# A hybrid GLA, differential-attention and PEER trunk: scores by map, value projection beside the key drain, GLA sums first and roots in pairs

## The chip, the cores and the metric

The kernel runs on one core of one Trainium2 chip. The metric is the time of one execution in device microseconds; the median of three runs is given. One execution was also taken with the profiler.

## What is computed

One layer of a streaming encoder, float32, width 1024, for 1024 prompt tokens and 32 decode tokens (with 512 cached keys). Shared weights, two streams of conditioning.

```
h = rmsnorm(x) * gain * (1 + sc1) + sh1
gq, gk, gv, gr, glr, dq, dk, dv, gates = split(h @ w_in)
# mixer A: gated linear attention, 4 heads (dk 128, dv 256)
b = cumsum(log_sigmoid(glr @ w_alpha + b_alpha) / 16)
o_a = causal((q e^b)(k e^-b)^T) v + (q e^b) state;  state = e^b_last state + (k e^(b_last - b))^T v
y_a = (rmsnorm(o_a) * silu(gr)) @ w_gla_out
# mixer B: differential attention, 8 heads, two maps of 64 per head, values of 128
q, k = rope(rmsnorm(dq)), rope(rmsnorm(dk))       # k and dv are also outputs
p = softmax(q1 k1^T / 8, block-causal by 64) - lam * softmax(q2 k2^T / 8, same mask)
y_b = (rmsnorm(p v) * 0.8) @ w_diff_out
x = x + gt1 * ((sigmoid(g_a) y_a + sigmoid(g_b) y_b) @ w_out)
# PEER: per token 8 heads x top 16 of 128^2 experts by product keys
x = x + gt2 * sum_k softmax(score)_k gelu(h2 . u[idx_k]) v[idx_k]
```

## The kernel before, in words

The nine token tiles (eight of 128, one of 32) form five groups: tile 0, then tiles 1-2, 3-4, 5-6 and 7-8. For each group a *lane* of ticks runs all layers up to the product keys: norm, key projection and rotation ("dk"), value projection ("dv"), two passes of GLA with two heads each ("gq", "gk", "la", "gv", "gla", "gr"), query projection ("dq"), attention ("at"), merge, output projection, second norm and product keys. After that each token needs 128 expert rows. They come in 528 batches of two gathers, 1 MB each, into a ring of nine slots: `dots(b)` on DVE (L1657) multiplies the rows with the tokens, ACT applies gelu (L1212), `weigh(b)` makes a diagonal on DVE (L1668) and sums on PE (L886), which frees the two slots for POOL's next gathers (L1711).

`ticks(g)` lists the lane of a group with a cost for each tick. `sequence()` places them: the whole lane of group 0 and the first 14 ticks of group 1 (`EARLY`) stand ahead of the first gather, the latter beside the expert selection of tile 0; then come the two `unit` items (SP fetches a unit's tokens and indices) and the batches. The lane of group g+1 is spread over the batches in proportion to its costs: group 1 over batches 0 to 47, group 2 over 48 to 167, and so on; the last 120 or so batches have no lane beside them. `order(engine)` turns that into one program order for each engine, so every engine, SP's DMA queue too, takes the ticks in the same order and waits in place for its semaphores. PE has the lane's ticks and then `weigh(b-1)`; DVE `dots(b)`, `weigh(b-1)`, then the ticks; ACT half of the ticks, `dots(b)`, the rest.

The parts that the change touches:
- *Ticks* (L162 to 167). A dk tick i makes one projected tile on PE (`tokens`, L624) while i < 4 nt (nt tiles in the group); the square is on ACT a tick later (L986), the rotation's sums on DVE (L1339 to 1359), root and scaling (L1367) one and two later, PE's transposes (L660) one more, ACT's copies (L1006) and SP's stores (L1797 the rotated keys, L1808 their transpose) after that. So there are six ticks without a projection (the drain). A dv tick makes one tile on PE (L624), a copy on ACT (L1016), two stores. Weights lie in three slots of 1 MB; when the last tile of a unit is done, SP issues the load of three units later (L1737) and waits for PE first.
- *Banks.* PE takes PSUM banks 0 to 5 in turn (`take`, ALL). A GLA output goes to bank 2 or 5.
- *Scores* (`attend` on PE, L795). Map 0 reads partitions 0 to 63, map 1 partitions 64 to 127, each into its own two banks (`pair[m]`). Where a unit or the one before has more than 512 keys ("wide", every unit of groups 2 to 4), the scores wait for the exponentials of the unit just before; else for those of one earlier. Keys come in chunks of 512. DVE then sets a corner to a large negative number (L1503) and takes the maximum (L1504) of each map; ACT takes the exponentials (L1151).
- *GLA* on ACT: tick k copies the transposed key of unit k-2 (L1079), squares the output of unit k-3 (L1087), takes Ln and Exp of its mean (L1090, L1091: the root), then the decays of unit k (L1107 to L1112). On DVE: scaling of unit k-4's output by the root (L1405), which frees its bank, state update of k-3 (L1413), mask of k-2 (L1419), keyed products of k-1 (L1429 to 1434), and last the running sum of unit k (L1440, L1443). On PE: outputs and state product of k-2 (L715, L716, L721), the block products of k-1 (L729) and a transpose (L734). A stage has 2 nt units (in group 4: two units of tile 7, then two of tile 8) and four more ticks.

## Time and profile before

| | |
|---|---|
| median of 3 runs | 4257.27 us (4254.24 to 4258.38) |
| the profiled execution | 4264.31 us |
| its span, first to last instruction | 4262.5 us |
| mean granted TensorE clock | 0.802 of full |
| busy: PE, DVE, ACT, POOL | 3112.3, 2708.3, 1513.0, 1253.3 us |
| moved by DMA | 1499 MB, of which the gathers 1107 MB |
| mean DMA rate | 352 GB/s |

Busy times are averages over very different stages. Until 440 us nothing is gathered; then the lanes of groups 1 to 4 run beside the batches, at some 12 us per batch for group 1 and 7 us for the others; the last stretch has gathers alone, at some 5 us per batch. A releaser is what ended the idle time before an instruction.

### The profile page before, as it was taken

To read this page: it belongs to the slowest core of one execution; us is meant where nothing else is said; L and a number is where in the kernel's file an instruction comes from. 1 tells how busy PE (TensorE), PEld (TensorE's weight loads), DVE (VectorE), ACT (ScalarE), POOL (GpSimd) and SP (SyncE) were. 2 spreads that over 40 slices of the span, in tenths; PEclk is the share of its full clock that TensorE was granted. 3 is DMA by queue.
4 is the path that set the end of the run, shared out by engine and by line. 5 is a ranking of instruction groups with operands and counts; after the bars stand their busy time and mean duration, and the time that the engine had idled before them with its cause. 6 is when DMAs were issued, how large, how long until landed. Compare 5 with 4: busy or idle time off the path is not lost. (4 is left out here: it accounts for less than half of the span.)

```text
span 4262.5 us, 48896 instructions
## 1 busy us (share of the span) xinstructions
PE 3112.3 (73%) x15864; PEld 1989.7 (47%) x15864; DVE 2708.3 (64%) x7617; ACT 1513.0 (35%) x3085; POOL 1253.3 (29%) x1068
## 2 busy tenths in 40 slices
PE   6787688898788769788887679788776676633333
PEld 4676565676555327555554347454442364400000
DVE  1326357437667884578568874596678845776775
ACT  3533366312255651113555540133456611010010
POOL 0000112112233332333233332333333323354453
PEclk8798888899888779899878789888787788855555
DMA  7485767788989989999889899999999999999997
GB/s 263 142 323 188 285 237 260 270 312 336 361 342 373 359 313 398 394 417 404 352 353 361 335 368 385 414 399 400 382 387 383 373 414 413 396 415 415 414 404 329
DMA packets 269366, 1499.19 MB, mean 352 GB/s; under 512 B 44969, under 2 KB 81673, under 8 KB 97465
## 3 DMA queue, kind: packets, MB, share of 16 engines
q0 software_dynamic: 152064, 1107.36, 65.1%
q1 hardware_dynamic: 117048, 388.70, 24.2%
q8 instruction: 128, 2.10, 0.2%
q14 instruction: 126, 1.02, 0.1%
HBM read 1463.49 MB, written 31.36 MB: 351 GB/s over the span
## 5 line engine op out<-in xcount | busy, mean ns | idle before, releaser
L1711 POOL DMA_INDIRECT rt_ring<-in_peer_uv,rt_few_idx x1056 | 1250.0, 1184 | 2979.8 <-PE rt_acc L886 2344.6
L1657 DVE SCALAR_TENSOR_TENSOR rt_ring<-rt_ring,rt_h 128x1024 f32<-128x1024 f32 x1056 | 1267.6, 1220 | 541.2 <-DMA rt_ring<-in_peer_uv,rt_few_idx 536.6
L886 PE MATMUL rt_acc<-rt_ring,rt_diag 128*32 128x512 f32 x4224 | 762.4, 797 | 602.3 <-DVE rt_diag L1668 600.4
L635 PE MATMUL pair<-dense,w 128*128 128x256 f32 (+2 forms) x3056 | 599.4, 355 | 25.8 <-DMA w<-in_weights 24.2
L635 PEld LDWEIGHTS pair<-dense,w 128*128 128x128 f32 x3056 | 518.2, 198 | 140.7 <-issue 62.9
L624 PE MATMUL pair<-w,dense 128*128 128x256 f32 (+1 forms) x2352 | 557.8, 395 | 7.0 <-DVE dense L1313 2.8
L1212 ACT ACTIVATE rt_act_dot<-rt_dot 128x2 f32<-128x2 f32 x528 | 106.0, 202 | 1271.7 <-DVE rt_ring L1657 1262.5
L886 PEld LDWEIGHTS rt_acc<-rt_ring,rt_diag 128*32 128x32 f32 x4224 | 100.9, 122 | 930.1 <-DVE rt_diag L1668 789.3
L624 PEld LDWEIGHTS pair<-w,dense 128*128 128x128 f32 (+1 forms) x2352 | 437.5, 189 | 159.1 <-issue 73.7
L1668 DVE TENSOR_SCALAR rt_diag<-cst,rt_act_dot,rt_few_prob 128x32 f32<-128x32 f32 x1056 | 266.2, 297 | 82.6 <-ACT rt_act_dot L1212 64.1
L635 PE MATMUL bank<-dense,w 128*128 128x256 f32 (+2 forms) x1424 | 276.0, 350 | 1.4 <-DMA w<-in_weights 0.9
L635 PEld LDWEIGHTS bank<-dense,w 128*128 128x128 f32 x1424 | 236.1, 193 | 57.0 <-issue 31.5
L624 PE MATMUL bank<-w,dense 128*128 128x256 f32 (+1 forms) x1104 | 261.6, 394 | 0.2 <-DVE dense L1405 0.2
L624 PEld LDWEIGHTS bank<-w,dense 128*128 128x128 f32 (+1 forms) x1104 | 204.5, 188 | 67.9 <-issue 29.0
L1212 ACT ACT_TABLE_LOAD x171 | 219.4, 1283 | 3.0
L795 PE MATMUL pair<-w,dense 64*128 64x512 f32 (+5 forms) x416 | 124.8, 722 | 107.2 <-ACT dense L1151 99.7
L729 PE MATMUL pair<-dense 128*128 128x16 f32 (+1 forms) x528 | 98.8, 334 | 89.0 <-DVE dense L1434 89.0
L815 PE MATMUL bank<-w,dense 128*128 128x128 f32 (+2 forms) x640 | 130.6, 360 | 29.7 <-DVE dense L1472 28.3
L729 PEld LDWEIGHTS pair<-dense 128*128 128x128 f32 (+1 forms) x528 | 101.2, 289 | 105.3 <-issue 102.5
L815 PEld LDWEIGHTS bank<-w,dense 128*128 128x128 f32 (+2 forms) x640 | 107.8, 245 | 69.8 <-issue 67.4
L1151 ACT ACTIVATE dense<-pair,negmax 128x128 f32<-128x128 f32 (+8 forms) x144 | 104.8, 731 | 65.8 <-PE bank L770 47.4
L795 PEld LDWEIGHTS pair<-w,dense 64*128 64x128 f32 (+1 forms) x416 | 47.7, 235 | 158.8 <-issue 156.4
(241 smaller groups left out, 3314.5 us busy)
## 6 DMA issues: line engine op xcount, KB each, us to landing
w<-in_weights SPq DMA_DIRECT2D x284, 1024.0 KB
rt_ring<-in_peer_uv,rt_few_idx POOLq DMA_INDIRECT x1056
dense<-scratch_mod SPq DMA_DIRECT2D x18, 512.0 KB, 11.0
dense<-in_x_prompt SPq DMA_DIRECT2D x16, 512.0 KB, 10.3
rt_h<-scratch_h SPq DMA_DIRECT2D x33, 128.0 KB
rt_x<-scratch_x SPq DMA_DIRECT2D x132, 32.0 KB
out_k_prompt<-dense SPq DMA_DIRECT2D x32, 128.0 KB
out_v_prompt<-dense SPq DMA_DIRECT2D x32, 128.0 KB
```

The costliest lines, as they stand in the source:

```text
L624: mm = nc.tensor.matmul(bank[b][0:n, 0:CH], src[:, k, c0:c0 + n], wt[:, k * CH:(k + 1) * CH], start=(k == 0), stop=(k == KC - 1))
L635: mm = nc.tensor.matmul(bank[b][:, 0:n], wt[:, k * CH + j * P:k * CH + (j + 1) * P], src[:, k, 0:n], start=(k == 0), stop=(k == KC - 1))
L729: mm = nc.tensor.matmul(bank[b][0:n, i * GBLK:(i + 1) * GBLK], k_blk[:, i, 0:n], e_blk[:, x % 2, i * GBLK:(i + 1) * GBLK], start=True, sto ...
L795: mm = nc.tensor.matmul(pair[m][0:n, o + c:o + c + w], qd[rows, h, c0:c0 + n], keys_of[rows, c:c + w], start=True, stop=True)
L815: mm = nc.tensor.matmul(bank[5][0:n, 0:VD], mixT[0:w, G % 2, (kt - first) * P:(kt - first) * P + n], v[0:w, kt, :], start=(kt == 0), stop= ...
L886: mm = nc.tensor.matmul(acc[u % 2][a * T:(a + 1) * T, :], diag[b % 2][:, i, :], slot[:, D + c * BANK:D + (c + 1) * BANK], start=(q == 0), ...
L1151: nc.scalar.activation(prob[0:n, x % 2, m, 0:nk], pair[m][0:n, o:o + nk], ACT.Exp, bias=negmax[0:n, x % 2, m:m + 1], accum_out=total[0:n, ...
L1212: nc.scalar.activation(act_dot[:, b % 2, :], dot[:, b % 2, :], ACT.Gelu).then_inc(gelued, 1)
L1657: dt = nc.vector.scalar_tensor_tensor(up, up, 1.0, h2[u % 2][:], ALU.mult, ALU.mult, accum_out=dot[:, b % 2, i:i + 1])
L1668: dg = nc.vector.tensor_scalar(diag[b % 2][:, i, :], stack, act_dot[:, b % 2, i:i + 1], few_prob[u % 2][:, q * B + i:q * B + i + 1], ALU.m ...
L1711: nc.gpsimd.indirect_dma_start(ring[n % RING][:], None, d["peer_uv"], bass.IndirectOffsetOnAxis(ap=few_idx[u % 2][:, c:c + 1], axis=0)).th ...
```

## The change

In `ticks`, all dk projections come first, then dv ticks and the six draining dk ticks alternate. A GLA output's bank is one of 2, 5 and 4 in turn. Scores are made map by map, each map waiting for its own exponential. On ACT the square of unit k-3 goes behind the decays of unit k, and Ln and Exp are made for two units at once. On DVE the running sum is first in the tick, and two units' outputs are scaled in every odd tick. The same instructions remain, apart from half of the Ln and Exp operations and their table loads. (The words "early requests" in the change's name refer to nothing in the diff.)

```diff
@@ -159,12 +159,12 @@
         for kind in ("modrow", "modcol"):
             out.extend(((kind, part), 0.5) for part in range(2))
     add("norm", nt + 2, 4.5)
-    for kind in ("dk", "dv"):
-        lag = 6 if kind == "dk" else 2
-        for i in range(4):
-            for ti in range(nt):
-                out.append(((kind, g, i * nt + ti), 3.6 if kind == "dk" else 3.0))
-        out.extend(((kind, g, 4 * nt + i), 1.0) for i in range(lag))
+    out.extend((("dk", g, i), 3.6) for i in range(4 * nt))
+    for i in range(max(4 * nt + 2, 6)):
+        if i < 4 * nt + 2:
+            out.append((("dv", g, i), 3.0 if i < 4 * nt else 1.0))
+        if i < 6:
+            out.append((("dk", g, 4 * nt + i), 1.0))
     for p in range(2):
         for kind in ("gq", "gk"):
             out.extend(((kind, g, p, j), 3.0) for j in range(2))
@@ -710,7 +710,7 @@
                     if x < 2 and t == NT:
                         pe.wait_ge(st_in, 16 * (p + 1))
                     v = gv[0:n, ti, j * GDV:(j + 1) * GDV]
-                    bo, before = take(("go", g, p, t, j), [(2, 5)[(base + x) % 2]])
+                    bo, before = take(("go", g, p, t, j), [(2, 5, 4)[(base + x) % 3]])
                     pe.wait_ge(bank_free[bo], before)
                     nc.tensor.matmul(bank[bo][0:n, 0:GDV], attn[0:n, x % 2, 0:n], v, start=True, stop=False)
                     nc.tensor.matmul(bank[bo][0:n, 0:GDV], q_cum[:, x % 2, 0:n], s, start=False, stop=True).then_inc(bank_made[bo], 1)
@@ -782,16 +782,15 @@
                         slot = (g, "kv", kv_load_of(g, x))
                         keys_of = weights(slot)
                     wide = nk > BANK or (x > 0 and key_count(GROUPS[g][units[x - 1][1]]) > BANK)
-                    for m in range(2):
-                        pe.wait_ge(at_exped[m], base + max(0, x if wide else x - 1))
                     o = BANK * (x % 2) if nk <= BANK else 0
                     if x == 0:
                         b, before = sessions["dqT", g, 3, 1]
                         pe.wait_ge(bank_free[b], before + 1)
-                    for c in range(0, nk, BANK):
-                        w = min(BANK, nk - c)
-                        for m in range(2):
-                            rows = slice(m * HD, (m + 1) * HD)
+                    for m in range(2):
+                        rows = slice(m * HD, (m + 1) * HD)
+                        pe.wait_ge(at_exped[m], base + max(0, x if wide else x - 1))
+                        for c in range(0, nk, BANK):
+                            w = min(BANK, nk - c)
                             mm = nc.tensor.matmul(pair[m][0:n, o + c:o + c + w], qd[rows, h, c0:c0 + n], keys_of[rows, c:c + w],
                                                   start=True, stop=True)
                             if c + w == nk:
@@ -1077,18 +1076,6 @@
                     b, before = sessions["kt", g, p, t, j]
                     act.wait_ge(bank_made[b], before + 1)
                     nc.scalar.activation(k_tok[0:n, x % 2, :], bank[b][0:n, 0:P], ACT.Copy).then_inc(bank_free[b], 1)
-                if 0 <= k - 3 < len(units):
-                    x = k - 3
-                    ti, t, c0, n, j = units[x]
-                    c = x % 2
-                    b, before = sessions["go", g, p, t, j]
...
-                    act.wait_ge(gl_squared, base + x + 1)
-                    settle(nc.scalar.activation(gln[0:n, c:c + 1], gms[0:n, c:c + 1], ACT.Ln, bias=eps[0:n, :]))
-                    nc.scalar.activation(grstd[0:n, c:c + 1], gln[0:n, c:c + 1], ACT.Exp, scale=-0.5).then_inc(gl_rstd, 1)
                 if k < len(units):
                     ti, t, c0, n, j = units[k]
                     c = k % 2
@@ -1112,6 +1099,19 @@
                         ex = nc.scalar.activation(e_key[:, c, OFF[i]:OFF[i + 1]], cum[:, c, 1:GBLK * (i + 1) + 1], ACT.Exp,
                                                   scale=-1.0, bias=cum[:, c, GBLK * i:GBLK * i + 1])
                     ex.then_inc(gl_decays, 1)
+                if 0 <= k - 3 < len(units):
+                    x = k - 3
+                    ti, t, c0, n, j = units[x]
+                    c = x % 2
+                    b, before = sessions["go", g, p, t, j]
+                    act.wait_ge(bank_made[b], before + 1)
+                    act.wait_ge(gl_squared, base + x)
+                    nc.scalar.activation(gsq[0:n, :], bank[b][0:n, 0:GDV], ACT.Square, scale=GDV ** -0.5,
+                                         accum_out=gms[0:n, c:c + 1]).then_inc(gl_squared, 1)
+                    if c == 1:
+                        act.wait_ge(gl_squared, base + x + 1)
+                        settle(nc.scalar.activation(gln[0:n, :], gms[0:n, :], ACT.Ln, bias=eps[0:n, :]))
+                        nc.scalar.activation(grstd[0:n, :], gln[0:n, :], ACT.Exp, scale=-0.5).then_inc(gl_rstd, 2)
 
             def gla_gate(g, p, i):
                 nt, u = len(GROUPS[g]), i - 1
@@ -1397,8 +1397,18 @@
                             dve.wait_ge(kt_out[i], 16 * (g + 1))
                         settle(nc.vector.memset(k_blk, 0.0))
                         settle(nc.vector.memset(cum, 0.0))
-                if 0 <= k - 4 < len(units):
-                    x = k - 4
+                if k < len(units):
+                    ti, t, c0, n, j = units[k]
+                    c = k % 2
+                    if k >= 2:
+                        dve.wait_ge(gl_decays, base + k - 1)
+                    settle(nc.vector.tensor_tensor_scan(cum[:, c, 1:n + 1], one[:].to_broadcast([P, n]), glT[:, j, c0:c0 + n],
+                                                        0.0, ALU.mult, ALU.add))
+                    start = cum[:, c, 0:n].rearrange("p (b c) -> p b c", c=GBLK)[:, :, 0:1].to_broadcast([P, n // GBLK, GBLK])
+                    nc.vector.tensor_tensor(blk[:, c, 0:n].rearrange("p (b c) -> p b c", c=GBLK),
+                                            cum[:, c, 1:n + 1].rearrange("p (b c) -> p b c", c=GBLK), start,
+                                            ALU.subtract).then_inc(gl_blocked, 1)
+                for x in range(k - 5, k - 3) if k % 2 == 1 and 0 <= k - 5 < len(units) else ():
                     ti, t, c0, n, j = units[x]
                     b, before = sessions["go", g, p, t, j]
                     dve.wait_ge(gl_rstd, base + x + 1)
@@ -1432,17 +1442,6 @@
                         w = GBLK * (i + 1)
                         nc.vector.tensor_tensor(k_blk[:, i, 0:w], gkT[:, j, c0:c0 + w], e_key[:, c, OFF[i]:OFF[i + 1]], ALU.mult)
                     nc.vector.tensor_tensor(e_end[:, c, 0:n], kk, e_end[:, c, 0:n], ALU.mult).then_inc(gl_keyed, 1)
-                if k < len(units):
-                    ti, t, c0, n, j = units[k]
-                    c = k % 2
-                    if k >= 2:
-                        dve.wait_ge(gl_decays, base + k - 1)
-                    settle(nc.vector.tensor_tensor_scan(cum[:, c, 1:n + 1], one[:].to_broadcast([P, n]), glT[:, j, c0:c0 + n],
-                                                        0.0, ALU.mult, ALU.add))
...
             def gla_gate(g, p, i):
                 nt, u = len(GROUPS[g]), i - 1
```

## Rows read from the trace of the kernel before

**Rows 1.** Six stretches: us; PE, PEld, DVE, ACT, POOL busy; granted clock; DMA share; GB/s

```profile
0.00:440.00 440.00, 321.94 (x2076) 267.45 (x2076) 157.92 (x605) 167.21 (x363) 3.36 (x12) 0.84 0.62 223
440.00:1031.00 591.00, 510.72 (x2452) 382.96 (x2452) 295.65 (x907) 241.20 (x512) 107.65 (x103) 0.89 0.77 288
1031.00:1912.00 881.00, 694.72 (x3368) 456.91 (x3368) 607.74 (x1711) 336.06 (x679) 274.81 (x240) 0.85 0.93 366
1912.00:2831.00 919.00, 726.55 (x3560) 476.45 (x3560) 641.43 (x1757) 366.96 (x710) 292.45 (x256) 0.85 0.95 374
2831.00:3720.00 889.00, 652.09 (x3520) 382.15 (x3520) 631.89 (x1731) 352.42 (x687) 313.04 (x256) 0.82 0.98 394
3720.00:4262.00 542.00, 206.28 (x888) 23.79 (x888) 373.63 (x912) 49.17 (x134) 262.04 (x201) 0.50 0.97 395
```

**Rows 2.** Timeline of group 0's key drain: start us, us, instruction [idle before <-releaser]

```profile
60.09 0.43 SPq L1797 DMA_DIRECT2D out_k_prompt<-dense  x1
...
65.21 0.43 DVE L1359 TENSOR_TENSOR dense<-dense 128x256 f32<-128x256 f32 x1 [3.79 <-DMA out_k_prompt<-dense]
...
66.22 1.11 PE L660 MATMUL pair<-cst,dense 128*128 128x128 f32 x4 [6.32 <-DVE dense L1367]
...
69.87 0.69 PE L660 MATMUL bank<-cst,dense 128*128 128x128 f32 x2 [2.53 <-DVE dense L1367]
...
70.35 15.09 PE L624 MATMUL pair<-w,dense 128*128 128x256 f32 x64
```

**Rows 3.** Group 1's key drain: one stretch as in rows 1, then lines of the timeline

```profile
427.00:452.00 25.00, 0.06 (x1) 0.00 (x0) 12.43 (x15) 3.82 (x5) 9.50 (x9) 0.51 0.50 166
...
411.20 3.62 PE L624 MATMUL pair<-w,dense 128*128 128x256 f32 x16
...
452.38 0.69 PE L660 MATMUL pair<-cst,dense 128*128 128x128 f32 x2 [25.32 <-issue]
```

**Rows 4.** GLA stages: table loads of L1090, a wait over the run, lines of the timeline

```profile
L1090 ACT ACT_TABLE_LOAD  x36: 1283/1283/1283, 122.0 to 3140.5; - x36
...
DVE dense L1405 <- ACT grstd L1091: 32.6, 15, 3.8
...
170.64 1.06 PE L716 MATMUL bank<-state,dense 128*128 128x256 f32 x2
...
172.35 4.93 PE L624 MATMUL bank<-w,dense 128*128 128x256 f32 x16
...
540.41 0.42 DVE L1440 TENSOR_TENSOR_SCAN dense<-one,dense 128x128 f32<-128x128 f32 x1
...
547.03 1.22 PE L721 MATMUL pair<-dense 128*128 128x256 f32 x2 [1.25 <-ACT dense L1079]
```

**Rows 5.** Stretches as in rows 1: group 2's keys, the attention of groups 2 and 3

```profile
1031.00:1106.00 75.00, 47.38 (x226) 31.00 (x227) 70.65 (x201) 31.34 (x57) 19.31 (x16) 0.80 0.77 284
1413.00:1598.00 185.00, 116.41 (x558) 54.15 (x562) 156.34 (x403) 103.96 (x185) 62.41 (x52) 0.73 0.86 324
...
2283.00:2525.00 242.00, 155.24 (x751) 76.99 (x750) 200.86 (x494) 139.55 (x222) 85.98 (x70) 0.75 0.88 338
```

**Rows 6.** Wide attention: lines of the timeline, and DVE's waits for scores, 1413 to 3420

```profile
1515.01 1.35 PE L795 MATMUL pair<-w,dense 64*128 64x512 f32 x8 [1.63 <-ACT dense L1151]
...
2324.46 1.00 ACT L1151 ACTIVATE dense<-pair,negmax 128x896 f32<-128x896 f32 x1
...
2325.69 2.93 PE L795 MATMUL pair<-w,dense 64*128 64x512 f32 x8 [2.88 <-ACT dense L1151]
...
2328.67 0.11 DVE L1503 MEMSET pair<- 64x64 f32 x1 [4.32 <-PE pair L795]
2328.81 0.96 DVE L1504 TENSOR_REDUCE negmax<-pair 128x1 f32<-128x768 f32 x1
...
2339.26 3.34 PE L795 MATMUL pair<-w,dense 64*128 64x512 f32 x8 [2.77 <-ACT dense L1151]
...
DVE pair L1503 <- PE pair L795: 51.5, 28, 4.5
```

More of the change, by code:

```diff
@@ L1079, in gla @@
                     nc.scalar.activation(k_tok[0:n, x % 2, :], bank[b][0:n, 0:P], ACT.Copy).then_inc(bank_free[b], 1)
-                if 0 <= k - 3 < len(units):
-                    x = k - 3
-                    ti, t, c0, n, j = units[x]
-                    c = x % 2
-                    b, before = sessions["go", g, p, t, j]
-                    act.wait_ge(bank_made[b], before + 1)
-                    act.wait_ge(gl_squared, base + x)
-                    nc.scalar.activation(gsq[0:n, :], bank[b][0:n, 0:GDV], ACT.Square, scale=GDV ** -0.5,
-                                         accum_out=gms[0:n, c:c + 1]).then_inc(gl_squared, 1)
-                    act.wait_ge(gl_squared, base + x + 1)
-                    settle(nc.scalar.activation(gln[0:n, c:c + 1], gms[0:n, c:c + 1], ACT.Ln, bias=eps[0:n, :]))
-                    nc.scalar.activation(grstd[0:n, c:c + 1], gln[0:n, c:c + 1], ACT.Exp, scale=-0.5).then_inc(gl_rstd, 1)
                 if k < len(units):
@@ L1434, in gla @@
                     nc.vector.tensor_tensor(e_end[:, c, 0:n], kk, e_end[:, c, 0:n], ALU.mult).then_inc(gl_keyed, 1)
-                if k < len(units):
-                    ti, t, c0, n, j = units[k]
-                    c = k % 2
-                    if k >= 2:
-                        dve.wait_ge(gl_decays, base + k - 1)
-                    settle(nc.vector.tensor_tensor_scan(cum[:, c, 1:n + 1], one[:].to_broadcast([P, n]), glT[:, j, c0:c0 + n],
-                                                        0.0, ALU.mult, ALU.add))
-                    start = cum[:, c, 0:n].rearrange("p (b c) -> p b c", c=GBLK)[:, :, 0:1].to_broadcast([P, n // GBLK, GBLK])
-                    nc.vector.tensor_tensor(blk[:, c, 0:n].rearrange("p (b c) -> p b c", c=GBLK),
-                                            cum[:, c, 1:n + 1].rearrange("p (b c) -> p b c", c=GBLK), start,
-                                            ALU.subtract).then_inc(gl_blocked, 1)
             def gla_gate(g, p, i):
```

## Prediction

> **What bounds the kernel now.** I read the stretches first [rows 1]. Up to 440 us (group 0, before the first gather) the DMA queues are busy 0.62 of the time and PE 322 of 440 us; while the lane of group 1 runs (440 to 1031) PE is busy 511 of 591 us at a DMA share of 0.77. Both are paced by PE and by what PE waits for, so a microsecond of PE idle time removed there is a microsecond of the program. In the lanes of groups 2, 3 and 4 the DMA share is 0.93, 0.95 and 0.98, and in the tail 0.97: there bytes decide, and only the stretches that lie under 0.9 can give anything. Next I read where PE stands still around the key projection [rows 2, 3], then the GLA stages [rows 4], then the wide attention of groups 2 and 3 [rows 5, 6].
>
> **Value ticks among the draining key rotation.** No instruction is added or removed. In group 0 PE waits 6.32 and 2.53 us for the rotated keys before two of its transposes, and only then starts the four value tiles, 15.09 us for 64 entries [rows 2]. With the new order value tiles 0 to 3 stand between these transposes. That would hide 8.9 us, but SP is a queue that the step is moved past: the weight load released by value tile 0 now stands ahead of the store of the first rotated keys, issued at 60.09 today. The load waits until tile 0 has run (59.7 + 3.6 = 63.3), so the store goes out 3.3 us later, and the DVE sum that waits for that store (65.21 [rows 2]) moves to about 68.5. PE then has tiles 0 and 1 until 67, waits some 2.5 us, and ends at about 78 in place of 85.4. I take 7 us, between 4 (the load's wait repeats at the next tile) and 9.
>
> In group 1 the drain lies in the start of the gathers: PE is idle 25.32 us before the last key transposes, because the DVE scaling that it waits for stands behind the first gathered rows; in 427 to 452 PE is busy 0.06 of 25 us [rows 3]. New: value tile 0 takes the place of a key tick in the early part, and tiles 1 to 3 come in the first batch's ticks, all ahead of the waiting transposes. A tile is 16 entries, 3.62 us at full clock [rows 3]. Four tiles are 14.5 us moved into the hole, two are 7.2. Weights for three of the four value loads are there, the fourth's load stands behind the two unit items of SP (about 450), and the gathers then fill nine slots, so some of the lead is lost to weights. I take 10 us, bounds 4 and 14.5. In group 2 the same waits exist at a DMA share of 0.77 over 75 us, 17 us of DMA idle [rows 5]: 3 us, bounds 0 and 7. Groups 3 and 4 run this at a share near 1 [rows 1]: nothing. Sum 20.
>
> **GLA: running sums first, roots in pairs, three banks.** Today each of the 36 units loads a table before its Ln and another before its Exp: 36 loads of 1283 ns at L1090 and as many at L1091 (the same count; one is shown) [rows 4]. Pairs leave 18 of each: 46 us of ACT time gone. ACT is not the bound, so I read what waits for it: PE waits 1.25 us for the key copy in the fourth unit of group 1, where ACT came late because a root stood ahead of the decays, and DVE waits 32.6 us in all, 15 times, for a root [rows 4]. The head of each stage, where nothing is pipelined, stays as it is. Moving the sums costs nothing: DVE waits at that point anyway; without this cover each would cost its own 0.42 us [rows 4] and the subtraction behind it. I take 1.5 us for each of the six four-unit stages of groups 1 to 3, 9 us, bounds 0 and 15; group 4 has two-unit stages at a high DMA share: 0. Against it stands one wait. With three banks the second GLA stage of group 0 puts its first output in bank 4, which the first gate tile takes (it started at 172.35 [rows 4]), and that output is now freed only when the pair has its root: the second output is ready at 171.7 (1.06 us from 170.64 [rows 4]), then come its square, two loads of 1.28 and three small operations, some 4.1 us, so 175.8. That is 3.5 us of PE on the fill's path: 3 us lost. In group 3 the bank of the first gate tile is also one that is held, but the DMA share covers it. Net 6.
>
> The Trainium skill ("ScalarE: Activation LUTs", Table sets: the hidden batching unit) says that Ln followed by Exp needs one load, since one set has both. By it a pair would save one load, 23 us of ACT instead of 46, and the stages perhaps 5 us instead of 9. The trace does not agree: two loads per unit, each 1283 ns.
>
> **Scores map by map.** This matters only where a unit or its predecessor has over 512 keys: 48 units, 16 in each of groups 2 to 4. Before: both maps wait for the second exponential; then PE takes 2.93 us (768 keys) or 3.34 us (896), and DVE, which had waited 4.32 us, clears and takes the two maxima one after the other, 0.96 us for 768 keys and about 1.1 with the clearing [rows 6]. DVE waits like this 28 times for 51.5 us [rows 6]. The two maps run side by side now: 640 keys of two maps took 1.35 us [rows 6], while 16 entries of 256 columns, 2048 columns, took 3.62 us [rows 3]; one behind the other 1280 columns would be 2.26. From 2.93 and 3.34, 128 more keys cost 0.41 us in the slow level (1.2 GHz), a chunk of 512 so 1.64 and about 0.82 at 2.4 GHz; the granted mean is 0.73 to 0.75, half the time each [rows 5].
> New: map 0 starts one exponential earlier, 1.00 us for 896 keys [rows 6]. If matmuls start in program order, the first chunk of map 1 waits for the second chunk of map 0 to start, so it runs 1.64 - 1.0 = 0.64 us late in the slow level and not late in the fast one; 0.32 us on average. DVE has the first maximum out of the way by then and ends 1.1 - 0.32 = 0.8 us earlier, while the apply and the weighing behind it on PE come 0.32 us later. Over 32 units of groups 2 and 3: 25 us of DVE, of which about 0.7 is where DVE really waits: 18 us, less 4 for the late weighing. DMA idle in these two windows is 0.14 x 185 + 0.12 x 242 = 55 us [rows 5], room enough. I take 14, bounds -10 and 25, and nothing in group 4. In groups 0 and 1 the wait was for an older exponential: nothing; the added wait is covered because it is long satisfied.
>
> The Trainium skill ("TensorE: Matmul & The Clock Gate", Part 3: Packing small matmuls - row/col tiling) says that matmuls never pass one another, only weight loads do. By it the sum is the one given; if the halves of the array kept queues of their own it would be some 14 us better. No row here has two chunks of one map in a row, so the trace does not decide.
>
> **Sum.** 7 + 10 + 3 + 6 + 14 = 40 us. The profiled execution took 4264.3 us (span 4262.5) and would take 4224; it stood 7 us above the median of 4257.27, so the median becomes 4217.
>
> **Rivals.** (a) *Maps on their own:* map 1 starts when its exponential is done, whatever stands ahead. For it: the pairs of today start together; against: the rule of program order. Then 1.1 us per unit on DVE and no late weighing: 14 more, 4203. (b) *The DMA absorbs it:* from 1031 on the share is 0.93 to 0.98, and gathers that start earlier only queue. Then groups 0 and 1 alone count: 7 + 10 + 3 - 3 = 17, 4240. (c) *The hole stays:* SP or the weights hold the value tiles back; what is left is -3 + 9 and a part of the attention, some 8 us: 4249. (d) *Slower:* changing the order of chunks ends the overlap altogether, in the wide score ticks of PE. Then 896 keys take 3.34 us more in the slow level, 1.0 of it paid by the early start, half of that in the fast level: 1.2 us per unit, 40 units of two chunks, 47 us of late weighings, against which 26 us of the rest stand: 4278. It decides from about 0.65 us of lateness per unit. For it: the pace of PE and the ring meet exactly there; against: DVE, not PE, is what the ring waits for.
>
> **How the numbers follow.** Forecast 0.45, own range 4200 to 4235; (a) 0.20; (b) 0.17; (c) 0.11; (d) 0.07. The range 4185 to 4247 leaves out (d) and half of (c). A measurement of this kernel tells about 0.2% (8.5 us) from no change: faster, below 4248.8, 0.82 (forecast, (a) and (b)); the same 0.11 (c); slower 0.07 (d).
>
> **What would show it.** Right: PE's wait of 6.32 us gone or under 3 us and value tiles between the key transposes near 60 us; four value tiles inside the 25 us hole; L1090 and L1091 loads 18 each; DVE's first maximum starting before the second map's scores end, its waits for scores well under 51.5 us; the second gate of group 0 near 176 us; the first gather near 436 us (7 - 3 earlier), the start of group 2's lane some 17 us earlier. Wrong: scores of 896 keys stretching to 5 us or more with POOL waiting longer, the windows of groups 2 and 3 unchanged in length, or a new PE wait for weights after 455 us.

## The result, and the profile after

The changed kernel takes 4215.11 us (median of 4 runs, 4210.74 to 4219.4), the kernel before, beside it, 4257.83: a ratio of 0.9902, with a 95% interval of 0.9887 to 0.9917. In a second series the same two stood at 4214.94 and 4261.01, 0.9892 (0.9871 to 0.9913). The forecast was 4217. The total came out as said; of the three parts that it was added up from none did, as the runs below show.

| | before | after |
|---|---|---|
| profiled span, us | 4262.5 | 4209.6 |
| ScalarE instructions | 3085 | 3014 |
| wait of DVE for a GLA root, us (times) | 32.6 (15) | 6.8 (3) |
| waits of DVE's clearing for scores, batches 100 to 384, us (times) | 51.5 (28) | 29.3 (23) |
| waits of PE for weights in L635, us | 25.1 | 56.1 |

The stretches of [rows 1], cut in the changed kernel at the same places of the work (same columns):

```profile
0.00:434.00 434.00, 333.30 (x2140) 277.99 (x2140) 157.93 (x605) 162.02 (x356) 3.36 (x12) 0.86 0.63 226
434.00:1009.40 575.40, 489.35 (x2388) 364.88 (x2388) 294.40 (x906) 227.98 (x495) 107.78 (x103) 0.90 0.78 296
1009.40:1878.00 868.60, 685.51 (x3368) 455.35 (x3368) 607.40 (x1712) 327.45 (x665) 279.58 (x240) 0.86 0.94 372
1878.00:2779.70 901.70, 719.77 (x3560) 472.12 (x3560) 641.14 (x1758) 354.76 (x694) 291.62 (x256) 0.86 0.96 382
2779.70:3668.00 888.30, 672.25 (x3524) 396.15 (x3528) 632.89 (x1734) 340.31 (x671) 306.64 (x257) 0.80 0.98 394
3668.00:4209.00 541.00, 205.47 (x888) 23.60 (x880) 372.75 (x906) 48.98 (x133) 260.21 (x201) 0.51 0.97 395
```

Against [rows 1] the first two stretches are 6 and 16 us shorter, the next two 12 and 17, the last two are as long as before. Where PE paced the program and where the DMA share lay under 0.97 there was something to win; at 0.97 and 0.98 there was nothing. (In the profiles the gain is 53 us, in the medians 43: the profiled execution of before stood 7 us above its median, that of the changed kernel 4 us below.)

The fill and the hole of group 1, lines of the timeline of the changed kernel (start us, us, instruction [idle before <-releaser]), against [rows 2, 3]:

```profile
61.96 3.62 PE L624 MATMUL pair<-w,dense 128*128 128x256 f32 x16
62.30 0.43 SPq L1796 DMA_DIRECT2D out_k_prompt<-dense  x1
67.77 0.43 DVE L1359 TENSOR_TENSOR dense<-dense 128x256 f32<-128x256 f32 x1 [7.59 <-DMA out_k_prompt<-dense]
68.78 0.44 PE L660 MATMUL pair<-cst,dense 128*128 128x128 f32 x2 [3.21 <-DVE dense L1367]
...
416.77 7.07 PE L624 MATMUL pair<-w,dense 128*128 128x256 f32 x32
424.12 3.62 PE L624 MATMUL bank<-w,dense 128*128 128x256 f32 x16
427.57 3.62 PE L624 MATMUL pair<-w,dense 128*128 128x256 f32 x16
446.93 1.12 PE L660 MATMUL pair<-cst,dense 128*128 128x128 f32 x4 [15.74 <-issue]
462.06 5.41 PE L624 MATMUL bank<-w,dense 128*128 128x256 f32 x16 [4.96 <-DMA w<-in_weights]
```

Four value tiles stand in the hole, whose wait falls from 25.32 to 15.74 us. Behind it PE waits 4.96 us for weights: SP issued their load at 445.25, behind the unit items, and it landed at 462.01.

The GLA stages and the wide scores, against [rows 4, 5, 6]: a group of the costliest instructions, two waits (total, times, longest), two stretches, and lines of the timeline.

```profile
L1113 ACT ACT_TABLE_LOAD x18 | 23.1, 1283 | 0.3
...
DVE dense L1415 <- ACT grstd L1114: 6.8, 3, 2.8
...
162.82 10.17 PE L624 MATMUL bank<-w,dense 128*128 128x256 f32 x32 [3.50 <-DVE dense L1415]
...
DVE pair L1502 <- PE pair L794: 29.3, 23, 3.6
...
1387.00:1566.00 179.00, 120.58 (x559) 59.89 (x562) 156.58 (x405) 104.60 (x188) 63.04 (x52) 0.76 0.89 340
2244.00:2472.00 228.00, 160.09 (x750) 78.87 (x742) 200.76 (x495) 139.04 (x222) 82.57 (x70) 0.77 0.92 361
...
2322.28 0.19 ACT L1151 ACTIVATION_READ_ACCUMULATOR dense<-pair,negmax 128x1 f32 x1
2322.62 3.91 PE L794 MATMUL pair<-w,dense 64*128 64x512 f32 x8 [1.38 <-ACT dense L1151]
2323.16 0.20 ACT L1151 ACTIVATION_READ_ACCUMULATOR dense<-pair,negmax 128x1 f32 x1
2323.41 0.53 PEld L794 LDWEIGHTS pair<-w,dense 64*128 64x128 f32 x3 [0.33 <-ACT dense L1151]
2326.02 0.11 DVE L1502 MEMSET pair<- 64x64 f32 x1 [2.96 <-PE pair L794]
```

Map 0's scores start 0.15 us after its own exponential has ended (2322.47), map 1's load 0.05 us after the second one (2323.36), long before map 0's scores are through, and DVE begins to clear the corner for its first maximum 0.5 us before the scores end at 2326.53. The two attention windows are 6 and 14 us shorter. The wait of 3.50 us at 162.82 is the bank that the prediction named.

### The profile page after: what moved, and what is told of

It is laid out like the page before. It is cut to its first block and busy times, and to the rows that moved or that the text cites. A ratio compares the mean times of both kernels' runs of the same rounds, so it can differ in the third digit from the quotient of the medians.

```text
span 4209.6 us, 48838 instructions
## 1 busy us (share of the span) xinstructions
PE 3105.7 (74%) x15864; PEld 1990.1 (47%) x15864; DVE 2706.5 (64%) x7617; ACT 1461.5 (35%) x3014; POOL 1249.2 (30%) x1068
## 3 DMA queue, kind: packets, MB, share of 16 engines
q14 instruction: 125, 1.02, 0.1%
## 5 line engine op out<-in xcount | busy, mean ns | idle before, releaser
L635 PE MATMUL pair<-dense,w 128*128 128x256 f32 (+2 forms) x3056 | 598.7, 355 | 37.8 <-DMA w<-in_weights 36.0
L635 PEld LDWEIGHTS pair<-dense,w 128*128 128x128 f32 x3056 | 518.4, 199 | 151.0 <-issue 62.0
L624 PE MATMUL pair<-w,dense 128*128 128x256 f32 (+1 forms) x2320 | 547.0, 393 | 5.8 <-DVE dense L1313 2.8
L624 PEld LDWEIGHTS pair<-w,dense 128*128 128x128 f32 (+1 forms) x2320 | 427.7, 188 | 151.7 <-issue 68.9
L635 PE MATMUL bank<-dense,w 128*128 128x256 f32 (+2 forms) x1424 | 283.3, 356 | 20.5 <-DMA w<-in_weights 20.1
L635 PEld LDWEIGHTS bank<-dense,w 128*128 128x128 f32 x1424 | 242.4, 198 | 79.1 <-issue 34.0
L624 PEld LDWEIGHTS bank<-w,dense 128*128 128x128 f32 (+1 forms) x1136 | 210.1, 188 | 75.4 <-issue 30.6
L794 PE MATMUL pair<-w,dense 64*128 64x512 f32 (+5 forms) x416 | 153.5, 680 | 63.1 <-ACT dense L1151 57.3
L729 PE MATMUL pair<-dense 128*128 128x16 f32 (+1 forms) x528 | 87.7, 311 | 91.8 <-DVE dense L1444 91.8
L729 PEld LDWEIGHTS pair<-dense 128*128 128x128 f32 (+1 forms) x528 | 89.7, 260 | 109.4 <-issue 106.9
L794 PEld LDWEIGHTS pair<-w,dense 64*128 64x128 f32 (+1 forms) x416 | 66.5, 222 | 130.1 <-issue 120.3
```

The costliest lines, as they stand in the source:

```text
L624: mm = nc.tensor.matmul(bank[b][0:n, 0:CH], src[:, k, c0:c0 + n], wt[:, k * CH:(k + 1) * CH], start=(k == 0), stop=(k == KC - 1))
L635: mm = nc.tensor.matmul(bank[b][:, 0:n], wt[:, k * CH + j * P:k * CH + (j + 1) * P], src[:, k, 0:n], start=(k == 0), stop=(k == KC - 1))
L729: mm = nc.tensor.matmul(bank[b][0:n, i * GBLK:(i + 1) * GBLK], k_blk[:, i, 0:n], e_blk[:, x % 2, i * GBLK:(i + 1) * GBLK], start=True, sto ...
L794: mm = nc.tensor.matmul(pair[m][0:n, o + c:o + c + w], qd[rows, h, c0:c0 + n], keys_of[rows, c:c + w], start=True, stop=True)
```

## Where each part pays: the three parts one at a time

Three kernels, each the one before with one part of the diff alone.

**Ticks.** The hunk in `ticks(g)` alone.

> The kernel before with the new order of ticks alone (dk projections first, then dv ticks and draining dk ticks in turn). By the prediction's own terms 7 + 10 + 3 = 20 us less than before, a ratio of 0.9953. Theory A, from the profile after: the fill gives 9 (its 5.8 at the first batch plus the 3.5 that the bank wait costs, which this kernel does not have), the hole some 8, and group 2 nothing, so 17 us, 0.996. Rival B: the hole's lead is lost again to weights (the wait of 4.96 us at 462 and the DMA share near 1 behind it) and only the fill's 9 us stay: 0.998. In A the first block products of group 1 (L729) start about 17 us earlier than before, in B about 9.

Measured 4251.93 us (4246.36 to 4260.51), before 4261.22: ratio 0.9979 (0.9968 to 0.999), 9 us. The first block products of group 1 start 15 us earlier (512.90 against 527.94), near theory A's 17, but of that only B's 9 are left at the end.

**Scores.** The hunk in the scores alone.

> The kernel before with scores map by map alone. By the prediction's term 14 us less than before (0.9967), all in the attention windows of groups 2 and 3. Theory A, from the profile after: the second map starts at its own exponential beside the first map's chunk, so the windows of groups 2 and 3 shorten by about 6 and 14 us and group 4's by 2: 22 us, 0.9948. Rival B: part of the shortening of those windows came from gathers that stood better after the other parts: 10 us or less, 0.998. No change before 1413 us in either.

Measured 4238.06 us (4230.1 to 4246.98): 0.9946 (0.9927 to 0.9964), 23 us, as theory A has it.

**Recurrence.** The hunks in the GLA stages alone (order, pairs, three banks).

> The kernel before with the GLA parts alone: three output banks, squares behind the decays, paired roots, running sums first. By the prediction's term 6 us less than before (0.9986): 9 won in six stages, 3 lost to the bank in the fill. Theory A, from the profile after: the stages of group 1 shortened by about 7.6 and 4 us, those of group 2 by 3.8 and 3.7, group 3's by 3 together, less 3.5 in the fill: 18 us, 0.9957. Rival B: group 1's first stage only gave back lead that the hole had won (its batches fall at other places), so alone it is as predicted: 6 us. In A the first gate matmuls of group 1 start 4 us or more earlier than before, in B at most 1.

Measured 4232.12 us (4229.56 to 4241.13): 0.9933 (0.9916 to 0.995), 29 us, more than theory A's 18. The first gate products of group 1 start 5.5 us earlier (552.30 against 557.82), of which the fill brought 2.

Alone they gain 9, 23 and 29 us, 61 in all, against 43 to 46 together. The stages of the profiles say where. Batch n begins with DVE's first product on its gathered rows; the table gives by how many us it begins earlier than in the profile of before (a minus: later). The kernel without ticks comes below.

```
batch         0     12     48     68    126    220    255    end
changed     5.8   21.7   21.1   18.4   32.2   38.7   52.9   52.9
ticks       6.3   16.1   11.6    8.8   10.0   12.4   13.2   13.3
scores     -2.4   -2.5   -2.3   -2.8    2.3   12.9   25.4   24.5
GLA         2.0    5.5    3.7    6.9   15.0   26.3   29.5   31.6
no ticks   -3.0    6.2   10.3   11.3   31.2   42.5   60.1   61.4
```

Each row is one execution; that of the kernel without ticks was 16 us faster than its median, so its row reads high towards the end. The ticks lead by some 16 us from batch 12 to 36. They lose 4 between batches 36 and 40, still in group 1's lane: there DVE waits for a read of the modulation rows (`scratch_mod`), 5.5 us (L1558) where it was 1.3 before, since the same read took 13.4 us to land (922.00 to 935.43) in place of 9.3. The wait is 5.5 and 5.3 us in both profiles of the changed kernel too, and absent in the kernel without ticks. They fall back to 9 at batch 68, in the key and value stretch of group 2. The other two gain mostly from group 2 on. So the term of the ticks was over, those of the scores and of the recurrence under what they are worth.

## The scores: the early start, not the order of the chunks

```
 s1:  for m: wait exped[m]          s2:  for c in chunks:
      for m:                                for m:
          for c in chunks: matmul               if c == 0: wait exped[m]
                                                matmul
```

> The changed kernel, but both exponential waits stand ahead of both maps again, and the chunks go map by map. Theory A (the gain of the scores is that map 1 starts at its own exponential): nearly all of the score part is lost, 20 to 25 us, so 4235 to 4240; the second map's first chunk starts when both exponentials are done, and the first chunk of map 0 is no earlier than before. Theory B (the gain is the order of the chunks, so that the maximum over map 0 can start while map 1 is scored): it keeps the time, 4213 to 4220.

Measured 4237.1 us (4227.36 to 4253.45), before 4262.01: 0.9943 (0.9924 to 0.9963).

> The changed kernel with the chunks of the two maps in turn, as before, but the wait for map 1's exponential only ahead of map 1's first chunk. Theory A (early start): keeps the time within 4 us, 4213 to 4220. Theory B (order map by map): gives back what the order brought, 14 us by the sum of the prediction, 4229. If both count, something between.

Measured 4224.74 us (4207.33 to 4225.55): 0.9908 (0.9891 to 0.9925).

In the same unit as above (timeline of s1) both maps wait for the second exponential, and the wait of DVE is back to nearly the 51.5 us of [rows 6]; the waits of DVE for the same stretch of s1, then s2:

```profile
2341.00 0.20 ACT L1152 ACTIVATION_READ_ACCUMULATOR dense<-pair,negmax 128x1 f32 x1
2341.34 2.05 PE L795 MATMUL pair<-w,dense 64*128 64x512 f32 x8 [2.26 <-ACT dense L1152]
...
DVE pair L1503 <- PE pair L795: 49.1, 25, 4.5
```

```profile
DVE pair L1503 <- PE pair L795: 31.1, 19, 4.4
```

Theory A holds in the main: without the early start 17 us go (0.9943 against 0.9902), with the early start and the old order of chunks only 0.0006 by the ratio, inside either interval. (The median of 4224.74 lies above theory A's 4220, in four runs that spread over 18 us, so a few us for the order aren't excluded.) Most of what the change gains here comes from the place of two waits; a gain from the order of the loops isn't measurable.

## The recurrence: order alone, pairs alone

```
 g1 (order only): roots and scaling for one unit at a time, as before
 g2 (pairs only): running sums last on DVE, squares and roots ahead of the decays on ACT, as before
```

> The changed kernel with its roots and scalings unit by unit again (36 pairs of table loads in place of 18), while the running sums first, the decays ahead of the squares and the three banks stay. Theory P (the gain of the recurrence is the table loads saved, 2.57 us for each of 18 pairs, of which the wait of VectorE shows all): 20 us or more of the part's 29 are lost, 4235 or more. Theory Q (the gain is the order: the running sums no longer stand behind the scaling that waits for the root): it loses 8 us or less, 4216 to 4223.

Measured 4242.35 us (4232.38 to 4246.64): 0.9944 (0.9929 to 0.9959).

> The changed kernel with the old order of the recurrence on both engines (running sums last on VectorE, squares and roots ahead of the decays on ScalarE), while roots and scalings stay in pairs and the banks stay three. Theory P (table loads): keeps most, loses 8 us or less, 4216 to 4223. Theory Q (order): loses 20 us or more, 4235 or more. If both of these kernels lose some 10 to 15 us, either part alone shortens the same wait and each is worth half.

Measured 4231.47 us (4221.83 to 4245.83): 0.993 (0.9912 to 0.9948).

Against the changed kernel's 0.9902 the first loses 18 us, the second 12. Neither P nor Q as stated: both losses lie between their bounds, and they sum to 30, the worth of the whole part. By the times, then, each half is worth its share (the order 11 to 12 us, the pairs 17 to 18) and the shares add up, with some 10 us of uncertainty on each difference. DVE's wait for the root, in the kernel with the order alone, then with the pairs alone (total, times, longest):

```profile
DVE dense L1414 <- ACT grstd L1113: 41.7, 16, 4.8
```

```profile
DVE dense L1404 <- ACT grstd L1091: 9.3, 5, 2.4
```

The order alone makes that wait longer than the 32.6 us of [rows 4]; the pairs take most of it away. From the first score product (L729) to the last state product (L721), the six four-unit stages of groups 1 to 3 take the times below; behind the sum stand the time in which PE is idle in them and their mean granted clock.

```
                                                  sum    idle  clock
before       28.6  24.9  30.2  30.1  31.5  32.2   177.5  14.4  0.62
order only   29.9  27.6  30.2  30.2  28.0  31.5   177.4  23.9  0.64
pairs only   27.1  24.4  26.8  30.7  27.9  30.4   167.3  14.7  0.65
GLA alone    25.6  25.2  24.5  27.1  26.6  28.6   157.6  11.3  0.68
changed      21.3  20.6  26.8  27.0  28.0  28.4   152.1   9.5  0.70
```

The changed kernel takes 25.4 us less in all, 4.2 per stage, where the prediction took 1.5. But PE's idle time shrinks by 4.9 us only, 0.8 per stage. The other 20 us are busy time: the same entries (704 before, 703 recorded after) take 143 us in place of 163, at a higher granted clock. In group 1's two stages it rose from 0.62 and 0.64 to 0.84 and 0.76; with the GLA part alone it stayed at 0.63 and 0.64 there. The GLA part alone gains 19.9 us in these stages, of its 29, and 3.1 of them in idle time. So most of this gain came with a higher clock, and what raised the clock (the shorter waits, or where the stages come to lie beside other work) isn't shown. In idle time neither the order nor the pairs alone gain anything; together they do.

The end of the first stage of group 3 shows how. Before:

```profile
2091.01 3.45 PE L729 MATMUL pair<-dense 128*128 128x16 f32 x16
2098.42 1.06 PE L721 MATMUL pair<-dense 128*128 128x256 f32 x2
```

and changed:

```profile
2060.00 1.86 PE L729 MATMUL pair<-dense 128*128 128x16 f32 x16
2063.90 0.59 PE L721 MATMUL pair<-dense 128*128 128x256 f32 x2
```

From the last scores to the last state product it was 7.4 us, now it is 3.9. PE runs the same entries in between, without an idle gap in either, so nothing there waited for a root: the 3.5 us are the clock, 1.06 against 0.59 us for two state products.

## The ticks: a lead paid back to the weights

PE's waits for weights in L635 rose from 25.1 to 56.1 us. The largest, near 1131, in the timeline of the changed kernel:

```profile
1102.54 4.83 SPq L1736 DMA_DIRECT2D w<-in_weights  x1
...
1114.08 1.06 PE L885 MATMUL rt_acc<-rt_ring,rt_diag 128*32 128x512 f32 x8
1117.42 4.79 SPq L1807 DMA_DIRECT2D scratch_kT<-dense  x1
...
1128.40 0.69 SPq L1736 DMA_DIRECT2D w<-in_weights  x1
1131.31 8.95 PE L635 MATMUL bank<-dense,w 128*128 128x256 f32 x32 [16.16 <-DMA w<-in_weights]
```

The last value product ends at 1114, in the kernel before at 1142: 28 us ahead, of which the group brought 21 with it and the ticks added 7. But the next product, for which a new weight must come, starts at 1131.31 against 1144.35: 13 us ahead. The load that it waits for is not the one of 1128.40 but that of 1102.54. The semaphore that the product at 1131.31 waits for is that load's, and its sixteen updates come from 1129.77 to 1131.26; the load of 1128.40 has another semaphore and lands at 1136.51. So the weight took 28.7 us from issue to landing. SP's order cost it only some 6 us ahead of that: its slot was free at about 1096, and SP was issuing two stores until 1102.5. The wait of 17.17 us in group 3 is alike: issued at 1952.52, landed at 1983.15. In the kernel before, the load for the same product was issued at 1126.24 and landed at 1144.31, 18.1 us: the new one is issued 24 us ahead and lands 13 us ahead. All the while SP issues stores of keys and values, 4.79 us for one of keys. In the kernel before the last store of keys took

```profile
1108.94 0.56 SPq L1808 DMA_DIRECT2D scratch_kT<-dense  x1
...
1157.73 2.50 PE L635 MATMUL pair<-dense,w 128*128 128x256 f32 x5 [5.21 <-DMA w<-in_weights]
```

0.56 us, ahead of all value stores, and at a DMA share of 0.72 (1095 to 1110). Four kernels in one series ask what these waits cost and whose they are.

> The changed kernel itself, beside the three that follow: 4210 to 4222, and the same weight waits of PE in the lanes of groups 2 and 3 (16.16 us near 1131, 17.17 near 1983) if they belong to the order of the work and not to that one execution.

Measured 4214.94 us (4200.27 to 4226.19), before 4261.01: 0.9892 (0.9871 to 0.9913). The waits are 15.89 and 16.67 us (loads of 30.6 and 30.2 us), so they belong to the order of the work.

**Weights ahead of stores**

```
+ ahead = kind in ("dk", "dv")
+ if ahead: load_weights for finished(item)
  stages[kind](*args)             # its stores
- load_weights for finished(item)
```

> The changed kernel, but in the key and value ticks SP issues the weight load of a finished slot ahead of the stores of the same tick, not behind them. Theory S (the new weight waits, 35 us in groups 1 to 4 against 13 before, come from SP's own order: the load stands behind value and key stores that take 2 to 8 us each to issue): the waits near 1131 and 1983 fall from 16 and 17 us to under 8, and the time to 4195 to 4207. Theory D (the transfers themselves are late, since the DMA engines are full there, and the issue order only decides which of them is late): less than 4 us is won, 4211 to 4218, and the waits stay or turn up at the gathers.

Measured 4213.95 us (4203.59 to 4216.77): 0.9881 (0.986 to 0.9901), the same as the changed kernel. SP and PE in its timeline:

```profile
1104.06 3.57 SPq L1736 DMA_DIRECT2D w<-in_weights  x1
...
1126.75 6.93 SPq L1807 DMA_DIRECT2D scratch_kT<-dense  x1
1133.73 2.52 SPq L1736 DMA_DIRECT2D w<-in_weights  x1
...
1136.71 3.63 PE L635 MATMUL bank<-dense,w 128*128 128x256 f32 x8 [13.90 <-DMA w<-in_weights]
```

The wait is 13.90 us, the time is in theory D's range, and so theory S fails and D holds: the transfer itself is late. The load for this product is issued at 1104.06, as soon as its slot is free, and lands at 1136.67, 32.6 us later, with the DMA engines full (share 1.02 from 1104 to 1137). But full engines aren't the whole of it: at the same share, loads in this stretch land after 14.7 to 23.3 us in the kernel before and after 17 to 23 us in that without ticks. What makes them later when key and value stores alternate is not shown. Whether a load on a queue of its own would come sooner, or merely push the gathers back, was not tried.

**Ticks in groups 0 and 1 only**

```
+ if g < 2:  (value ticks among the drain)
+ else:      (keys, then values, as before)
```

> The changed kernel with the value ticks among the draining key rotation only in groups 0 and 1; groups 2 to 4 have keys, then values, as before. If the drains of the later groups had nothing to fill (beside other work the ticks alone gained 16 us up to the lane of group 2 and nothing behind it) and the weight waits are their price, it is faster than the changed kernel by up to 22 us, 4193 to 4210. If the price is hidden by the gathers that run on meanwhile, it is the same within 4 us.

Measured 4205.81 us (4198.19 to 4208.85): 0.9872 (0.9854 to 0.9891). The waits of PE for weights, in the changed kernel, then here (L643 is L635 of the others):

```profile
PE pair L635 <- DMA w<-in_weights: 36.0, 5, 17.2
PE bank L635 <- DMA w<-in_weights: 20.1, 2, 16.2
```

```profile
PE pair L643 <- DMA w<-in_weights: 25.6, 6, 10.3
PE bank L643 <- DMA w<-in_weights: 1.3, 1, 1.3
```

29 us of waiting go and 9 us of time by the medians; the intervals of the two ratios overlap, so the 9 is likely, not certain. That the rest of the waits had been made up by gathers that ran on meanwhile is the natural reading, not a measured one.

**No ticks at all**

> The scores and the recurrence of the change without its ticks. Parts that add up: 23 and 29 us gained, 4206 at before 4258; then the ticks would be worth less than nothing in the joined kernel. Parts that share a wait: the joined kernel's 43 us less the 9 that the ticks gave alone, 4224; or, if the ticks and the recurrence's order fill the same hole in group 1, the same as the changed kernel, 4215.

Measured 4219.03 us (4202.94 to 4226.43): 0.9909 (0.9892 to 0.9926). In the joined kernel the ticks are worth 4 us by the medians (7 by the ratios), not measurable with certainty. The time lies midway between the expected 4215 and 4224 and decides for neither. The last line of the table above is this kernel: 11 us behind the changed kernel at batch 48, level at batch 126. So the lead of groups 0 and 1 is used up in group 2, in these two executions. The other two parts together gain 39 to 42 us, against 52 alone; that is inside the intervals, so their overlap isn't settled.

**The bank wait.** The version above, and group 0's outputs back in two banks:

```
- [(2, 5, 4)[(base + x) % 3]]
+ [(2, 5)[x] if g == 0 else (2, 5, 4)[(base + x) % 3]]
```

> The version with value ticks among the drain in groups 0 and 1 only, and the two output sums of group 0 back in banks 2 and 5, so that the first gate product after them finds bank 4 free. Bank theory: the wait of 3.5 us for the scaling near 163 is gone, the other bank waits of the trace stay as they are, and the first gather comes 2 to 4 us earlier; the time 4199 to 4207. Rival: the wait moves to the next product that needs the output, and the first gather stays within 1 us; the time 4203 to 4210.

Measured 4190.18 us (4186.7 to 4211.14), before 4258.69: 0.9856 (0.9831 to 0.9881). Its timeline, where the changed kernel waited 3.50 us:

```profile
162.49 8.44 PE L632 MATMUL bank<-w,dense 128*128 128x256 f32 x32
172.39 0.66 PE L755 MATMUL pair<-cst,dense 128*128 128x128 f32 x4 [1.46 <-DVE dense L1467]
```

The wait is gone and nothing takes its place: from the head of this stage (149.28) to L755 are 23.1 us, in the version without the bank edit 27.0 (146.65 to 173.63). That bears out the bank theory for the wait. But batch 0 did not come 2 to 4 us earlier; it came 2 us later: 5 us were lost between 84 and 120 to a lower clock (see below), and 3.5 more behind this stage. Of the 15 us between the two medians the bank accounts for the 3.9 of this stage at most; the intervals of the ratios, 0.9856 and 0.9872, overlap. The time is below what either theory gave. It is the fastest of all that ran, 61 us faster than the kernel before by the ratio.

## Why the prediction was right, and where it was not

The time, 4217 against 4215, is luck: its three parts were wrong by 9 to 23 us. Alone, the ticks gave 9 us where 20 were forecast, the recurrence 29 where 6 were, the scores 23 where 14 were, 61 in all; that they gain 15 to 18 less together, which no term of the sum had, brings it back to the 40 of the forecast.

- **Fill drain, 7 us, and the store's delay:** right. The DVE sum moved to 67.77 (forecast 68.5), PE waits 3.21 us, and the drain ends at 78.09, as said. Batch 0 came 5.8 us earlier (1.7 in the second profile); forecast, less the bank's 3, was 4. The first gather starts at 434.4 (438.3), where 436 was said. The second gate of group 0 does not start near 176 but at 162.82: the fill was 13 us ahead there, more than the drain explains; some 3 of them are the first GLA stage, which ran at a clock of 0.67 in place of 0.50.
- **Hole in group 1, 10 us:** right at first. Four tiles stand in it; the ticks alone win 9.8 us between batches 0 and 12. That some lead is lost to weights was said, and the wait of 4.96 us is that loss. The other 4 us, lost at batches 36 to 40 to the late read of the modulation rows, were not foreseen.
- **Group 2's drain, 3 us:** wrong, the step that failed. The key stretch has the same 75 us as before, and behind it come 16.16 and, in group 3, 17.17 us of waiting for weights. The prediction read DMA idle time of 0.23 x 75 us as room. It did not look at the stretch right behind it, where the DMA engines are full and a weight load takes 28.7 and 30.6 us to land. A new wait of PE for weights after 455 us was one of the prediction's own signs of being wrong, and it came. So the ticks are worth 9 us alone, not 20.
- **GLA, 6 net:** the mis-sized term. 4.2 us per stage, not 1.5, and 29 us for the part alone. As a count of PE's idle time the 1.5 was not too small but too large, 0.8 measured (0.5 with the part alone); what the sum left out is the clock, at which the same entries take 20 us less over six stages. It also treated the new order as a move that costs and brings nothing, and by the times it is worth 11 to 12 us. The bank's cost was exact: 3.50 us.
- **Scores, 14:** rival (a) describes what happens. Map 1 starts when its own exponential is done. The part alone gave 23, near (a)'s 28; its time of 4203 would have needed the 20 us of the ticks as well. (b) has a kernel of truth: nothing was won behind batch 255 in the changed kernel's profile. (d) did not occur: 896 keys take 3.91 us with the early start in place of 3.34, but DVE's waits fell by 22 us. The term had taken for granted that matmuls start in program order. The Trainium skill ("TensorE: Matmul & The Clock Gate", Part 3: Packing small matmuls - row/col tiling) has matmuls start and end in program order. The trace does not agree in their starts for these two row halves of the array: map 1's first load goes out at 2323.41, and of the scores the entries that have begun by 2323.5, then by 2323.8, are (count, ns, first and last start)

```profile
L794 PE MATMUL pair<-w,dense x2: 1187/1202/1216, 2322.6 to 2323.4; 64*128 64x512 f32 x2
...
L794 PE MATMUL pair<-w,dense x3: 1057/1187/1216, 2322.6 to 2323.6; 64*128 64x512 f32 x3
```

The second entry starts where the second exponential lets map 1 go (0.05 us behind it); in program order it would have been map 0's second pass, and map 1's first only the fifth. That the entry is map 1's is read from its releaser, since the entries don't name the map.

## What to carry to other kernels

Put each wait ahead of the first instruction that needs it: one wait moved gained 17 us, and the reordered loop it came with nothing that could be measured. Where a part of the work frees an engine earlier, read the *next* resource in the stretch behind it (here weight loads that take 28 to 33 us to land with the DMA full), and apply the reorder only to the stages that have a hole to fill. When a load is late, pair it with its own semaphore before blaming the last one issued. Split a stage that got shorter into idle time and clock: here waits were a fifth of it.

## What the runs showed of the hardware

- The time SP needs to issue a store can grow more than tenfold where the DMA engines are full: 0.38 to 0.56 us for a store of keys at a share of 0.72 (before, 1095 to 1110), 4.79 and 6.93 us for the same store at 1.02 (changed kernel and weights first, 1110 to 1130). It need not: in the kernel before, value stores issued at a share of 1.02 (1110 to 1130) took from 0.43 to 5.07 us.
- A weight load of 1 MB, some 8 us from issue to landing in the median of a run, took 27.8 to 32.6 us ahead of the long waits in three kernels with ticks in group 2 (ticks alone, changed, weights first), at a share of 1.02 to 1.03, and 14.7 to 23.3 us at that share in the kernel before.
- The granted clock in the fill differs between executions of almost the same instructions. The two profiles of the changed kernel have 0.83 and 0.63 from 100 to 130. After the same pause of PE of 8 us the stretch 100 to 130 has, in the version with ticks in two groups and in that with the bank edit:

```profile
100.00:130.00 30.00, 23.25 (x127) 20.60 (x128) 7.70 (x32) 11.41 (x37) 0.00 (x0) 0.80 0.22 73
...
115.90 3.69 PE L632 MATMUL pair<-w,dense 128*128 128x256 f32 x16 [0.67 <-DVE state L1431]
```

```profile
100.00:130.00 30.00, 25.54 (x104) 21.58 (x105) 7.71 (x32) 8.97 (x27) 0.00 (x0) 0.65 0.19 70
...
116.23 5.98 PE L632 MATMUL pair<-w,dense 128*128 128x256 f32 x16 [0.67 <-DVE state L1431]
```

0.80 against 0.65 (means of the two levels, 1.2 and 2.4 GHz), 3.69 against 5.98 us for sixteen entries: some 5 us of the fill are luck, as much as the terms of this study that lie there. Edits in a fill are to be judged by the waits in it, not by the start of what follows.
